# In the eighth head GpSimd spreads the decode values and scales the decode states, in place of VectorE

## What is computed

```
S_t = exp(g_t) (I - beta_t k_t k_t^T) S_{t-1} + beta_t k_t v_t^T,  o_t = S_t^T q_t.
```

## Time and profile before

| | us |
|---|---|
| median of 3 runs | 3120.02 |
| profiled execution, whole | 3127.17 |
| its span | 3125.2 |
| TensorE busy | 2853.7 (91%) |
| VectorE busy | 1680.2 (54%) |
| ScalarE busy | 858.5 (27%) |
| GpSimd busy | 0.2 (0%) |
| mean granted clock of TensorE | 0.949 |

### The profile page before, as it was taken

One profiled execution on the slowest core, in us unless ns is written; L12 is line 12 of the kernel. 1 busy time (PEld: TensorE's weight loads), 2 busy tenths in 40 slices (PEclk: granted clock), 3 DMA queues, 4 the chain that ended last, 5 costly groups with the idle time before them and its releaser, 6 DMA issues. The chain is left out here.

```text
span 3125.2 us, 47548 instructions
## 1 busy us (share of the span) xinstructions
PE 2853.7 (91%) x18652; PEld 2779.4 (89%) x18652; DVE 1680.2 (54%) x3140; ACT 858.5 (27%) x1907; POOL 0.2 (0%) x4
## 2 busy tenths in 40 slices
PE   5999999999776999999999999758839999999998
PEld 2999999999746999999999999658739999999997
DVE  4766677766344544444444553247867444444445
ACT  3544444444112311221111321025514111122111
POOL 0000000000000000000000000000000000000000
PEclk8999999999757999999999999869969999999999
DMA  3100111102113111111111113731231111111111
GB/s 112 55 17 28 29 35 36 36 16 82 61 47 106 41 54 41 54 40 44 50 40 51 44 55 102 47 90 55 79 117 41 54 41 40 54 40 54 40 41 55
DMA packets 102203, 165.99 MB, mean 53 GB/s; under 512 B 47081, under 2 KB 65809, under 8 KB 101604
## 3 DMA queue, kind: packets, MB, share of 16 engines
q1 hardware_dynamic: 59604, 142.35, 14.3%
q10 hardware_dynamic: 42464, 21.74, 3.5%
HBM read 134.63 MB, written 34.67 MB: 54 GB/s over the span
## 5 line engine op out<-in xcount | busy, mean ns | idle before, releaser
L1743 PE MATMUL psum<-x_hi,w_hi 128*128 128x352 f32 (+1 forms) x2128 | 685.5, 322 | 13.8 <-DVE w_lo L914 7.0
L1744 PE MATMUL psum<-x_lo,w_hi 128*128 128x352 f32 (+1 forms) x2128 | 680.9, 320 | 0.0
L1745 PE MATMUL psum<-x_hi,w_lo 128*128 128x352 f32 (+1 forms) x2128 | 677.7, 318 | 0.0
L1743 PE MATMUL psum<-u_hi,w_hi 128*128 128x352 f32 (+1 forms) x1632 | 524.8, 322 | 2.4 <-DVE u_lo L1717 2.4
L1744 PE MATMUL psum<-u_lo,w_hi 128*128 128x352 f32 (+1 forms) x1632 | 522.2, 320 | 0.0
L1745 PE MATMUL psum<-u_hi,w_lo 128*128 128x352 f32 (+1 forms) x1632 | 520.6, 319 | 0.0
L1743 PEld LDWEIGHTS psum<-x_hi,w_hi 128*128 128x128 f32 x2128 | 400.3, 188 | 17.8 <-DVE x L1432 8.7
L1744 PEld LDWEIGHTS psum<-x_lo,w_hi 128*128 128x128 f32 x2128 | 400.9, 188 | 0.7
L1745 PEld LDWEIGHTS psum<-x_hi,w_lo 128*128 128x128 f32 x2128 | 400.5, 188 | 0.0
L776 ACT ACTIVATE u_hi<-relu 128x352 fp32r<-128x352 f32 (+1 forms) x192 | 94.4, 492 | 1044.1 <-DVE relu L1463 1044.1
L1432 DVE TENSOR_TENSOR x<-x,psum 128x352 f32<-128x352 f32 x336 | 170.6, 511 | 363.7 <-PE psum L1745 363.7
(11 more groups left out here) (296 smaller groups left out, 3539.1 us busy)
## 6 DMA issues: line engine op xcount, KB each, us to landing
w_raw<-in_w SPq DMA_DIRECT2D x192, 512.0 KB, 3.7
scratch_att<-o_out ACTq DMA_DIRECT2D x48, 132.0 KB, 2.6
q_tile<-scratch_q SPq DMA_DIRECT2D x24, 256.0 KB, 3.0
merge<-scratch_att SPq DMA_DIRECT2D x8, 768.0 KB, 4.7
scratch_q<-q_stage ACTq DMA_DIRECT2D x24, 176.0 KB, 2.2
x<-in_x SPq DMA_DIRECT2D x8, 516.0 KB, 7.6
scratch_o_heads<-head_out ACTq DMA_DIRECT2D x8, 512.0 KB, 2.7
s_state<-in_s_rec_in ACTq DMA_DIRECT2D x2, 2048.0 KB, 10.0
```

The costliest lines, as they stand in the source:

```text
L1743: mm(out, whi, xh[:, k, cols], start=k == 0, stop=False)
L1744: mm(out, whi, xl[:, k, cols], start=False, stop=False)
L1745: done = mm(out, wlo, xh[:, k, cols], start=False, stop=k == kts - 1)
```

## The change

A block for GpSimd is added, and `samples_update` on VectorE loses the spread and the scale. GpSimd waits once for the reads of the states and for `s_rows_ready`; then, for each n, it spreads and scales. From n = 1 it waits for `s_update1_full`, the second matmul of n-1, since that has read `s_v_wide`. VectorE's add waits for GpSimd's scale (`s_scaled_ready`) in place of its own last instruction.

```diff
+    @block.gpsimd
+    def _(pool):
+        L = Lane(pool, sem)
+        pool.wait_ge(sem("s_reads_full"), L.next("s_reads_full"))
+        for n in range(HEADS):
+            if n == 0:
+                pool.wait_ge(sem("s_rows_ready"), L.next("s_rows_ready"))
+            else:
+                pool.wait_ge(sem("s_update1_full"), L.next("s_update1_full"))
+            pool.tensor_tensor(s_v_wide[:], b3(ident[0:HEADS * NS, n * NS:(n + 1) * NS], NS), o3(s_rows[:, 1], NS), ALU.mult
+            ).then_inc(sem("s_v_wide_ready"), L.add("s_v_wide_ready"))
+            new = s_state[n // 4][:, n % 4]
+            pool.tensor_tensor(new, new, b3(s_gate[:, 1, n], NS), ALU.mult
+            ).then_inc(sem("s_scaled_ready"), L.add("s_scaled_ready"))
...
             if n:
                 old = s_state[(n - 1) // 4][:, (n - 1) % 4]
-                v.wait_ge(sem(L.last), L.value(L.last))
+                v.wait_ge(sem("s_scaled_ready"), L.next("s_scaled_ready"))
                 for h in range(2):
                     v.wait_ge(sem(f"s_update{h}_full"), L.next(f"s_update{h}_full"))
...
-            if n < HEADS:
-                own = ident[0:HEADS * NS, n * NS:(n + 1) * NS]
-                v.wait_ge(sem("s_rows_ready"), L.next("s_rows_ready") if n == 0 else L.value("s_rows_ready"))
-                v.tensor_tensor(s_v_wide[:], b3(own, NS), o3(s_rows[:, 1], NS), ALU.mult
-                ).then_inc(sem("s_v_wide_ready"), L.add("s_v_wide_ready"))
-                new = s_state[n // 4][:, n % 4]
-                v.tensor_tensor(new, new, b3(s_gate[:, 1, n], NS), ALU.mult).then_inc(sem("dve_order"), L.add("dve_order"))
```

## The result

| | before | after |
|---|---|---|
| median of 5 runs on one chip, us | 3120.02 (3119.33 to 3121.54) | 3103.54 (3101.67 to 3105.82) |
| profiled execution, whole | 3127.17 | 3105.82 |
| its span | 3125.2 | 3104.0 |
| mean granted clock | 0.949 | 0.951 |
| from the copy to `s_rows` to the first reload behind the head | 121.29 | 102.99 |

The changed kernel is faster by about half a per cent: the ratio of the times is 0.9945, with a 95% interval of 0.9934 to 0.9956. The forecast was 3103.4. The last row of the table is the stretch that the change works on: from the start of ScalarE's copy to `s_rows` to the start of its first pass over the reloaded heads (L758).

What follows compares the result with a forecast made beforehand. TensorE waits on VectorE's spread and scale in the eighth head's serial chain. Savings of 14.4 us, less 0.5 for holds, plus 2.7 for the clock, give 16.6 us: median 3120.0 becomes 3103.4 us, range 3097 to 3111.

Steps and rivals of the forecast that it cites:

- n = 0: Before update 0 in the levels: TensorE's whole wait of 1.91 us goes, as GpSimd has 4.8 us for the spread.
- n = 1 to 3: Updates 1 to 3 in the levels: TensorE is released one spread earlier, 1.13 us each, 3.4 us; adds late next.
- Chunks 0 to 3: Recurrence: spread and scale leave the chain, saving 2.27 us in chunk 0 and 6.8 us in chunks 1 to 3.
- G: Time of one spread or scale on GpSimd: taken as 2.4 us, bounds 1.21 to 3.6, hidden under 3.4.
- The mutual hold: Levels 3 to 5: VectorE's two-SBUF-input product L1308 and GpSimd hold each other; 0 to 1.5 us lost, 0.5 taken.
- The clock: Level 4 and update 1 run at 2.4 GHz without the stand before update 0: 1.75 + 0.94, 2.7 us gained.
- The clock as before: Rival for the levels: the clock does not rise, gain 13.9 us, time 3106.1; chance 23%.
- A slow GpSimd: Rival in the recurrence: G over 3.4 us; at G = 4.5 the gain is 5.7 us, 3114.3; chance 10%.
- 2G + 0.57: Length in us of a recurrence chunk if G is over 3.4 us; 9.57 at G = 4.5.
- GpSimd holding all of VectorE: Rival: any VectorE instruction waits for GpSimd's pair; 3121.7 at G = 2.4, 3129.7 at 3.0; 3% no change, 3% slower.
- lost behind the head: Rival behind the head: the projection waits for a transfer instead, so the time is that of before; chance 4%.
- The clock stays up longer: Rival for the levels: the clock stays up beyond level 4, gain up to 24 us, 3096; chance 12%.

Runs made afterwards that it cites:

- the scale alone: Against the changed kernel: GpSimd scales the states, VectorE spreads the values again in the old place; 3117.9 us, ratio 0.9994.
- GpSimd reads all the time: Changed kernel plus five two-input 128x768 GpSimd instructions between spread and scale of n = 0 to 6; 3129.16 us (one run).
- the spread alone: Against the changed kernel: GpSimd spreads the values, VectorE scales the states again in the old place; 3108.46 us, ratio 0.9957.
- the spread alone, started late: The spread alone, but for n = 5 to 7 GpSimd's spread also waits until VectorE's scale is done; 3107.1 us, ratio 0.9954.
- the stand put back: Changed kernel plus seven sets of a scratch tile on GpSimd before the first spread, delaying update 0; 3108.76 us, ratio 0.9961.
- GpSimd writes only: Changed kernel plus three write-only sets of a scratch tile on GpSimd between spread and scale of n = 0 to 6; 3101.23 us (one run).
- scales early: Against the changed kernel: GpSimd scales n = 0 to 3 right after the reads, each later one behind the spread before it; 3102.56 us.
- no holds: Against the changed kernel: scales 0 and 1 right after the reads, 2 behind spread 2, the rest behind spreads 3 to 6; 3103.57 us, ratio 0.9942.

## Why the prediction was right, step by step

*n = 0.* Right: 1.97 us saved for 1.91, with no wait left. The spread took 1.89 us where 4.8 were free.

*n = 1 to 3.* Right in kind: the adds are what is late next, and updates 2 and 3 come 1.20 and 1.16 us earlier for 1.13 predicted. Update 1 gave 0.47, since the held product of level 4 takes the other 0.7.

*Chunks 0 to 3.* Right: 2.22 for 2.27, and 6.78 for 6.8. Chunk 4 of before was a fair copy of what chunks 1 to 3 became, to a hundredth of a microsecond. What the step did not say is that it holds only for both instructions together. Its working (so many instructions times 1.13 us) would have given half for one of them, and the two half moves gave nothing in chunks 1 to 3. It was right since, with both gone, VectorE does nothing with two SBUF inputs beside GpSimd's pair in a chunk.

*G, the time of one spread or scale on GpSimd.* Mis-sized on the safe side: 1.86 us from start to start, not 2.4. It lies between the one pass of VectorE (1.21) and the two passes taken. It changed the sum little, since GpSimd was hidden at either value; the room of 6.8 us for a pair sufficed at 6.0 and was overrun at 12.98. The estimate of 2.25 us drawn from the Trainium skill (GPSIMD Engine Reference, Performance versus the Vector engine) was nearer but also too long; the measured 1.86 decides.

*The mutual hold.* Sized well: 0.7 us for 0.5. Its places were right: level 3, hidden beside update 0, and level 4. Its length was not: the product lost 1.16 us in level 4 rather than 0.6, and 0.7 of that reached TensorE. The working had taken the product's place from the row of before, 4.2 us behind the update, where the clock is low, while its own clock term put level 4 at full clock. There the product comes 849.50 - 846.91 = 2.6 us behind the update, in the middle of GpSimd's scale; that G was too long by 0.5 us hid part of this error. The rule of the Trainium skill that the prediction weighed (SBUF — State Buffer, Who interferes with whom: two SBUF inputs on VectorE and reads on GpSimd exclude each other; mere writes do not, nor does a VectorE instruction with one SBUF input outside the 2-port perf modes that it lists) agrees with these rows: 2.44 and 2.39 us beside a read, 1.22 beside three sets, 0.69 for an add from PSUM beside a read. The prediction had left out the words on those modes. Whether the one `TENSOR_SCALAR` that was held (last section) ran in such a mode, no run here shows.

*The clock.* The direction and the cause were right, and shown by the run that put the stand back. The size was the term that failed: 4.5 us for 2.7. Level 4 and update 1 gave 2.13 of it. The rest came from where the prediction wanted nothing: level 5 (0.66 to 0.80, 1.15 us) and update 3 (3.58 to 2.44 us, 1.15). "The later gaps shrink only by 1.1 us of 3 to 5, so I take the 2.7 us of level 4 alone" is the step: gaps that shrink in part gave back part of the clock too. Level 5 is better taken together with update 1 ahead of it, since the low clock falls now on the one, now on the other. From the profiled execution of each run, in us (level 4 from its first matmul to the end of its last, the last column from the start of update 1 to the end of level 5):

| run | wait before update 1 | level 4 | update 1 and level 5 |
|---|---|---|---|
| before | 3.23 | 6.52 | 10.02 |
| the scale alone | 3.10 | 6.52 | 10.07 |
| GpSimd reads all the time | 3.83 | 4.88 | 10.02 |
| changed | 2.76 | 4.88 | 8.38 |
| changed, again | 2.76 | 4.88 | 9.96 |
| changed, third | 2.75 | 4.88 | 8.38 |
| the spread alone | 2.19 | 4.88 | 8.41 |
| the spread alone, started late | 2.19 | 4.88 | 8.40 |
| the stand put back | 2.07 | 7.16 | 8.41 |
| GpSimd writes only | 2.07 | 4.88 | 8.38 |
| scales early | 2.06 | 4.88 | 8.40 |
| no holds | 2.06 | 4.88 | 8.37 |

In these runs the gain goes with the shorter wait and not with level 4's clock: with level 4 slow and a short wait it is there (8.41), with level 4 at full clock and a long wait it is not (10.02). In between, at 2.76 us, the same kernel shows both, and what decides there stays open. Update 3 behaves alike: from its start to the next matmul it took 3.52 and 3.46 us behind waits of 3.23 and 3.10, and 1.88 to 2.37 behind waits of 2.07 to 2.19. In the recurrence the profiled execution shows no gain from the clock, as said; the changed kernel again had 0.6 us of it in chunk 0.

*From profile to median.* The stretch lost 18.3 us, the medians 16.5 here, and 18.6 and 14.8 in the two later groups. The forecast of 3103.4 met 3103.54 more closely than its terms deserve, and that was luck: the clock gave 1.8 us more than its term, the scatter of medians took about as much back. For the profiled execution, where the working really ended, it had 3110.6, and 3105.82 was measured.

*The rivals.* The clock as before (3106.1) fell with level 4 at 1.00. A slow GpSimd fell at 1.86 us; its mechanism, with the add waiting for the scale, is what the kernel with seven reading instructions showed, although there the engine's own time (12.98 us for seven instructions) rather than 2G + 0.57 set the chunk. So that rival's chunk at G = 4.5 would be nearer 9.0 than 9.57 us, an estimate from this run. GpSimd holding all of VectorE was refuted by `vz` and the adds at full speed beside it. In its working for G = 3.0, the 3.8 us for the levels are derived nowhere. Nothing was lost behind the head. "The clock stays up longer" was the nearest to the truth, in part: two more pieces ran faster, not all of them.

## What to carry to other kernels

Moving work of VectorE to GpSimd pays where VectorE stands on a serial chain and GpSimd has slack, even at 1.5 times the duration (1.86 us for 1.21), because only the chain is paid for. Before moving one of several such instructions, look at the inputs of those that stay: where one left behind reads two SBUF tiles beside the moved one, it is held for as long as the move saves, and two halves that each give nothing (here in chunks 1 to 3) can be a whole that gives 7 us; then move both, or start the helper behind it. Remove a stand of TensorE with the clock in mind: here a stand of 2.8 us cost 4.8. And compare the clock by the sum over a stretch and over several executions: its pieces moved by more than 1 us between executions of one kernel.

## What the runs showed of the hardware that was not expected

- The hold is for the running instruction alone and goes both ways: with five more reading instructions queued on GpSimd a product took 2.5 to 2.8 us, and a scale of GpSimd that started 0.46 us behind a product took 2.53 us for 1.89.
- A GpSimd instruction with two inputs of 128x768 elements took as long from start to start (1.86 us; 9.32 for five) as one of 128x1024. The two differ in how their inputs are laid out: the shorter one repeats whole rows of both inputs, the longer ones (spread and scale) repeat single elements of one of them. No run separates the causes.
- A `TENSOR_SCALAR` of 8 elements on VectorE, one SBUF input, took 1.09 us beside a reading GpSimd. So "one SBUF input" alone is no safe mark; the adds and `vz`, which also read PSUM, were never held, and two `TENSOR_REDUCE` of 128x512 with one SBUF input kept their 1.27 us beside GpSimd just before it. The hold of the `TENSOR_SCALAR` was seen once and not followed up.
